# Splitting the mixer's per-head matrix work into pieces placed between the tiles of the next head's projection blocks

## What is computed

```
q, v, zf, zb, g = split(h @ w_in, 5)           # q = silu(q); k = (1-lb) * sigmoid(-z); f = lb + (1-lb) * sigmoid(z)
cum    = cumsum(log f) inside chunks of 64     # 12 chunks
scores = tri * ((q * exp(cum - ref)) @ (k * exp(ref - cum)).T)        # inside a chunk
kv[n]  = (k * exp(last - cum)).T @ v           # one 128 x 128 product per chunk
s[n+1] = decay[n] * s[n] + kv[n]               # chain over the chunks, both directions
o      = scores @ v + (q * exp(cum)) @ s[n]
y      = o * rsqrt(mean(o*o) + eps) * gnorm * silu(g)
out    = y @ w_out
```

## Time and profile before

| | |
|---|---|
| time, median of 3 runs | 3496.42 us |
| the profiled execution | 3493.21 us, span 3491.5 us |
| TensorE busy | 3158.1 us (90%) |
| TensorE weight load busy | 2570.7 us (74%) |
| VectorE busy | 1861.7 us (53%) |
| ScalarE busy | 1387.5 us (40%) |
| mean granted TensorE clock | 0.947 |
| HBM traffic | 102 GB/s over the span |

### The profile page before, as it was taken

The page is one execution under the profiler, slowest core; times in us unless marked ns, Lnnn a source line. Parts: engine busy times, 40 slices in busy tenths (PEclk is TensorE's granted clock), DMA queues, the critical chain, the costliest instruction groups (busy, mean ns, idle before and its releaser), DMA issues.

```text
span 3491.5 us, 44906 instructions
## 1 busy us (share of the span) xinstructions
PE 3158.1 (90%) x16582; PEld 2570.7 (74%) x16582; DVE 1861.7 (53%) x2627; ACT 1387.5 (40%) x1905; POOL 116.1 (3%) x121
## 2 busy tenths in 40 slices
PE   5988888578996999899888999999998999889997
PEld 4777777467875888766776888878887778678886
DVE  6554555367985443678536534563446333454435
ACT  4445544446874222456314322342224332342222
POOL 0000000000000000043100000000000000000000
PEclk8999989698998999999998999999999999999998
DMA  4311211138992222221001222222222222123322
GB/s 170 127 55 57 70 54 54 37 120 337 390 359 83 96 96 96 85 71 61 23 2 61 96 96 96 102 88 97 93 95 97 73 73 90 50 71 103 101 97 73
DMA packets 98049, 357.66 MB, mean 102 GB/s; under 512 B 11008, under 2 KB 11392, under 8 KB 97536
## 3 DMA queue, kind: packets, MB, share of 16 engines
q1 hardware_dynamic: 92448, 334.54, 27.5%
q0 software_dynamic: 4176, 15.24, 1.2%
q10 hardware_dynamic: 1296, 6.11, 0.5%
HBM read 344.29 MB, written 11.56 MB: 102 GB/s over the span
## 4 chain that ended last, share of the span: by engine, by line
PE 78%; DVE 9%; ACT 7%; issue 4%; DMA 1%; POOL 0%; ACTq 0%; DVEq 0%; POOLq 0%
PE bank L281 20%; PE bank L282 19%; PE bank L283 19%; PE bank L1622 1%; PE bank L1624 1%; PE bank L1623 1%; PE gbank L920 1%; ACT whi L259 1%; PE bank L2603 1%; ACT L352 1%; DVE cum L1066 1%; PE gbank L902 1%; PE gbank L937 1%; PE bank L1651 1%; PE bank L1650 1%
## 5 line engine op out<-in xcount | busy, mean ns | idle before, releaser
L281 PE MATMUL bank<-h_hi_buf,whi 128*128 128x512 f32 x2320 | 929.5, 401 | 53.7 <-DVE h_lo_buf L450 33.9
L282 PE MATMUL bank<-h_lo_buf,whi 128*128 128x512 f32 x2320 | 912.6, 393 | 0.0
L283 PE MATMUL bank<-h_hi_buf,wlo 128*128 128x512 f32 x2320 | 911.0, 393 | 0.0
L259 ACT ACTIVATE whi<-raw 128x1024 fp32r<-128x1024 f32 x466 | 477.3, 1049 | 456.5 <-PE bank L283 402.3
L272 DVE TENSOR_TENSOR wlo<-raw,whi 128x1024 fp32r<-128x1024 f32 x444 | 533.4, 1221 | 138.6 <-ACT whi L259 71.8
L281 PEld LDWEIGHTS bank<-h_hi_buf,whi 128*128 128x128 f32 x2320 | 442.4, 191 | 167.5 <-DVE h_lo_buf L450 42.7
L282 PEld LDWEIGHTS bank<-h_lo_buf,whi 128*128 128x128 f32 x2320 | 442.2, 191 | 95.2 <-issue 5.3
L283 PEld LDWEIGHTS bank<-h_hi_buf,wlo 128*128 128x128 f32 x2320 | 441.4, 190 | 93.9
L281 PE MATMUL bank<-a_hi_buf,whi 128*128 128x512 f32 x960 | 377.1, 393 | 25.0 <-DVE a_lo_buf L3184 9.6
L282 PE MATMUL bank<-a_lo_buf,whi 128*128 128x512 f32 x960 | 375.7, 391 | 0.0
L283 PE MATMUL bank<-a_hi_buf,wlo 128*128 128x512 f32 x960 | 375.6, 391 | 0.0
(11 more groups left out here) (512 smaller groups left out, 3803.3 us busy)
## 6 DMA issues: line engine op xcount, KB each, us to landing
raw<-in_w SPq DMA_DIRECT2D x634, 512.0 KB, 3.4
x<-in_x ACTq DMA_DIRECT2D x2, 2048.0 KB, 10.8
sorted_rows<-zrow POOLq DMA_DIRECT2D x7, 514.0 KB, 8.4
xrow<-sorted_rows POOLq DMA_DIRECT2D x7, 514.0 KB, 7.5
sorted_y<-ysb POOLq DMA_DIRECT2D x7, 512.0 KB, 7.4
out<-x SPq DMA_DIRECT2D x8, 256.0 KB, 2.0
xc<-in_xc ACTq DMA_DIRECT2D x1, 1024.0 KB, 8.7
waup<-in_waup ACTq DMA_DIRECT2D x1, 256.0 KB, 5.2
```

The costliest lines, as they stand in the source:

```text
L259: act.activation(k.whi[:, g.slot, :], k.raw[:, g.slot, :], ACT.Copy).then_inc(k.split_hi, 1)
L281: pe.matmul(out, w_hi, hi, start=(t == 0), stop=False)
L282: pe.matmul(out, w_hi, lo, start=False, stop=False)
L283: return pe.matmul(out, w_lo, hi, start=False, stop=(t == tiles - 1))
```

## The change

1. **Pieces.** `pe_tokens` and `pe_states` are cut up: V turn, K turn forward, K turn backward, scores, states in three lots. The V turn stands between block 0 and the modulation block; the others are called from inside `pe_block`, between two tiles of QB, VB and GB. The output stays at the end of the turn.
2. **Norm one turn later.** A turn has a third head `f` = h-2. Its norm product stands inside block 0, its ScalarE and VectorE steps between the steps of head e. The gate is now multiplied in before the norm factor (`y_gated`). One more turn is written out ahead of the loop, one more (none, none, 7) behind it.
3. **Half rows.** `v_half` and its two copies are gone. The chunk product reads 64 rows of `ktok` and of `vtok`; the chunk's parity chooses the bank, and a lot holds both directions and signals once (N_KV 3, not 6).
4. **Order on VectorE and ScalarE.** Gate products go ahead of split 2, both scans ahead of the modulation reduce and split 3, kk and qq ahead of the take of ZB; the chain's first lot ahead of the take of VB. ScalarE makes all six sigmoids ahead of split 2, copies V after the logarithms, and split 6 goes ahead of the copies of K.

Core of the diff:

```diff
+        def at_first(t):
+            if h.n.reg is None and h.n.base == 0:
+                pe.wait_ge(k.h_ready, q.h - DC + t + 1)
+            if f is not None and t == 4:
+                self.pe_norm(k, q, f)
+        def at_query(t):
+            if e is not None and t in (4, 7):
+                self.pe_keys(k, e, 0 if t == 4 else 1)
+        def at_value(t):
+            if e is not None and t == 2:
+                self.pe_scores(k, e)
+            if e is not None and t == 6:
+                self.pe_states(k, e, 0)
+        def at_gate(t):
+            if e is not None and t in (0, 4):
+                self.pe_states(k, e, 1 if t == 0 else 2)
+        pe_block(k, g, DC, lat, more=(con, h.count(3, 0)), ready=at_first)
         if e is not None:
-            self.pe_tokens(k, e)
+            self.pe_values(k, e)
...
+        pe_block(k, g + QB, DC, lat, ready=at_query)
+        pe_block(k, g + VB, DC, lat, more=(con, h.count(3, 2)), ready=at_value)
+        pe_block(k, g + GB, DC, lat, ready=at_gate)
         if e is not None:
-            self.pe_output(k, q, e)
+            self.pe_output(k, e)
...
+    def pe_turn(self, k, e, n, src):
         pe = k.nc.tensor
+        for i, tiles in enumerate((range(4), range(4, 6))):
+            if n == 0:
+                wait(pe, k.o_taken, e.n)
+            else:
+                wait(pe, k.tok_copied, e.count(N_TOK, n + i - 1))
+            for j in tiles:
+                last = pe.transpose(k.gbank[i][:, (j - tiles[0]) * P:(j - tiles[0] + 1) * P], src(j), k.ident[:, :])
+            last.then_inc(k.gla_full, 1)
...
+    def pe_states(self, k, e, lot):
         pe = k.nc.tensor
+        if lot == 0:
+            wait(pe, k.tok_copied, e.count(N_TOK, N_TOK))
+            wait(pe, k.pt_ready, e.count(N_SC, N_SC))
+        else:
+            wait(pe, k.chain_step, e.count(2 * STEPS, 8 * lot))
+        for i, j in enumerate(range(4 * lot, min(4 * lot + 4, STEPS))):
+            for d in range(2):
                 c = CHAIN[d][j]
+                half = slice(CH * (c % 2), CH * (c % 2) + CH)
+                last = pe.matmul(k.gbank[c % 2][:, i * P:(i + 1) * P], k.ktok[half, d, c // 2, :], k.vtok[half, c // 2, :],
+                                 start=True, stop=True)
+        last.then_inc(k.gla_full, 1)
...
     def run(self, eng, k, q, iteration):
+        iteration(k, q, Head(0), None, None)
+        iteration(k, q, Head(1), Head(0), None)
+        iteration(k, q, Head(2), Head(1), Head(0))
+        with eng.Fori(0, HEADS - 3) as it:
+            iteration(k, q, Head(At(3, 1, it)), Head(At(2, 1, it)), Head(At(1, 1, it)))
+        iteration(k, q, None, Head(HEADS - 1), Head(HEADS - 2))
+        iteration(k, q, None, None, Head(HEADS - 1))
...
@@ act_iteration
+        if f is not None:
+            wait(act, k.o_taken, f.count(1, 1))
+            act.activation(k.osq[:, :], k.o32[:, :], ACT.Square).then_inc(k.osq_ready, 1)
...
+        if f is not None:
+            wait(act, k.norm_sum, f.n + (q.norm + 1))
+            act.activation(k.lnv[:, :], k.nbank[:, :], ACT.Ln, bias=k.eps_col[:, :], scale=1.0 / P).then_inc(k.ln_ready, 1)
+        if e is not None:
+            turned(0, k.vtok)
         split(3)
+        if f is not None:
+            wait(act, k.ln_ready, f.n + (q.norm + 1))
+            wait(act, k.y_ready, f.n)
+            act.activation(k.rstd[:, :], k.lnv[:, :], ACT.Exp, scale=-0.5).then_inc(k.rstd_ready, 1)
...
@@ dve_iteration
         split(2)
         if e is not None:
+            for d in range(2):
+                self.dve_scan(k, e, d)
         if h is not None:
             wait(dve, k.block_done, g + MOD_BLOCKS + 1)
             dve_mod(k, k.bank[1][:, 0:MOD_BLOCKS * P], MOD_BLOCKS, h.n.times(MOD_BLOCKS) + 2 * DC, 0,
...
         split(3)
...
+        take(ZB, k.z_st[:, 1, :], context=True)
+        split(4)
+        if f is not None:
+            wait(dve, k.rstd_ready, f.n + (q.norm + 1))
+            wait(dve, k.y_gated, f.count(1, 1))
+            dve.scalar_tensor_tensor(k.o32[:, :], k.o32[:, :], k.vec("gnorm")[:, 0:1], k.rstd[:, :], ALU.mult, ALU.mult
+                                     ).then_inc(k.y_ready, 1)
+        split(5)
...
+            self.dve_chain(k, e, 0)
         take(VB, k.v_st[:, :], context=True)
         if e is not None:
+            self.dve_chain(k, e, 1)
+            self.dve_chain(k, e, 2)
```

More of the change, by code:

```diff
@@ L861, in pe_iteration @@
         con = lambda t: k.hc[:, t, :]
[L862 to L870, removed]
@@ L871, in pe_iteration @@
-        if e is not None:
-            self.pe_tokens(k, e)
-        if h is not None:
-            pe_block(k, g + VB, DC, lat, more=(con, h.count(3, 2)))
-        if e is not None:
[L876 to L879, removed]
-            self.pe_output(k, q, e)
-    def pe_tokens(self, k, e):
-        pe = k.nc.tensor
[L885 to L897, removed]
+        if h is None:
+            if f is not None:
[3 more added lines that the diff above has]
+                for d in range(2):
+                    self.pe_keys(k, e, d)
+                self.pe_scores(k, e)
+                for lot in range(N_KV):
+                    self.pe_states(k, e, lot)
+                self.pe_output(k, e)
+            return
@@ L991, in act_iteration @@
         split(5)
+        split(6)
         if e is not None:
-            n = 0
             wait(act, k.exp_done, e.count(4, 4))
[L995 to L1008, removed]
+            turned(2, k.ktok[:, 0])
+        if f is not None:
+            wait(act, k.y_ready, f.count(1, 1))
+            act.activation(head_view(k.a_hi_buf, f.n), k.o32[:, :], ACT.Copy).then_inc(k.y_hi, 1)
+        if e is not None:
+            turned(4, k.ktok[:, 1])
+        split(7)
         if e is not None:
@@ new lines, in dve_chain @@
+    def dve_chain(self, k, e, lot):
+        dve = k.nc.vector
+        wait(dve, k.gla_full, e.count(G_HEAD, N_TOK + N_SC + lot + 1))
+        for j in range(4 * lot, min(4 * lot + 4, STEPS)):
+            for d in range(2):
+                if j > 0:
+                    wait(dve, k.chain_step, e.count(2 * STEPS, 2 * j + d - 1))
+                if j >= 5:
+                    wait(dve, k.state_copied, e.count(STATE_COPIES, 2 * (j - 5) + d + 1))
+                kv = k.gbank[CHAIN[d][j] % 2][:, (j % 4) * P:(j % 4 + 1) * P]
+                before = CHAIN[d][j - 1]
+                if j == 0:
+                    wait(dve, k.rho_done, e.count(2, 2))
+                    ins = dve.tensor_copy(k.xs[:, d, 0, :], kv)
+                else:
+                    ins = dve.scalar_tensor_tensor(k.xs[:, d, j % 2, :], k.xs[:, d, (j - 1) % 2, :],
+                                                   k.rho[:, d, before:before + 1], kv, ALU.mult, ALU.add)
+                ins.then_inc(k.chain_step, 1)
```

205 lines of the change are left out of this document (92 added, 113 removed).

## The result

The changed kernel takes 3371.5 us, median of four runs (3371.0 to 3376.4), against 3493.8 for the kernel before (four runs, 3488.2 to 3500.3): a ratio of 0.965 [0.963, 0.967]. The forecast was 3397 with a range of 3378 to 3420: the direction was right, the gain of 122 us was a quarter larger than the 99 I gave, and the time lies under the range.

What follows compares the result with a forecast made beforehand. TensorE and waits in its in-order work were taken to set the turn. Seven turns falling to 394.5 us (-93.4) and the tail (-6) took 3493.2 to 3393.8, or 3397 as median; range 3378 to 3420.

Steps and rivals of the forecast that it cites:

- part 2: States in half rows: 44 instructions at 0.107 us plus 0.2 for each of three pieces, 5.3 us a turn.
- the term for the half rows: States of a turn: 44 half-row instructions at 0.107 us each, without overlap, within 5.3 us.
- The second rival: States: half rows overlap, 2.35 us less a turn, 3381 us; chance 0.10 together with a better clock.
- The stall of 0.5: Waits of TensorE in a turn where margins are small: 0.5 us added, between 0 and 2.5.
- Three places with margins of 0.1 to 0.2: QB's weights, states lot 1 to 2, and lot 2 to output: not all hold, so 0.5 us a turn.
- Transposes and change-overs: In a turn, 18 transposes at 0.12, 2.2 us; changes from full-row f32 pieces back to blocks, 0.4 us.
- The margin at QB: Low part of QB's weights ready on VectorE at 22.3 us of the turn, wanted by TensorE at 22.5: 0.2.
- the 4.9 us set aside: Remainder of the old third turn of 69.68 us, put to half clock and restarts behind gaps.
- the end of -11: Tail, where only the last head's mixing is left: best case -11 us if its output gets full clock; -6 expected.
- VectorE's queue as the pace: Both scans ahead of QB's split make QB late every turn: 3411 us, 3425 with a clock dip; chance 0.22.
- The clock held down by f32 pieces: f32 pieces keep QB, VB, GB and output at 1.2 GHz: turn of 89 us, kernel about 3610; chance 0.03.
- Uncovered pieces: Waits inside the blocks as long as before, only moved: same turn, less the tail, 3490 us; chance 0.01.

Runs made afterwards that it cites:

- the first run above: Changed kernel with each lot of states issuing all products of the lower half of the rows, then all of the upper: 3388.8 us, 0.971 of the kernel before.
- the two copies: Changed kernel with two useless 512-column VectorE copies in every turn ahead of the low part of QB's weights: 3380.8 us, 0.967 of the kernel before.

## Why the forecast was right in its direction and too high

**The step that failed** is in part 2: "eight f32 instructions of 64 rows ... 0.86 us, 0.107 each" and the sentence built on it, "By the second the 44 would need 2.35; the 0.107 disagrees". The row has eight instructions and one shape, and I took it for eight of that shape. The line of the same instructions, asked by itself in the kernel before, shows two (min/median/max in ns, start, shapes):

```profile
L2121 PE MATMUL bank<-kv_a,q_a x8: 272/374/378, 1514.7 to 1515.3; 64*128 64x128 f32 x4, 64*128 64x256 f32 x4
```

Four of 128 columns and four of 256. As an estimate from the lots above, with overlap these are 4 x 0.056 + 4 x 0.11 + 0.2 for the first and last (1.09 - 16 x 0.056) = 0.86, which is what passed; without, 1.5. The row that disagreed with the Trainium skill (TensorEngine Tiling (Array Packing), Key Properties: tiles run matmuls in parallel) in truth agreed with it, and the first run above shows it with nothing but an order changed: pairs every 0.112 us against single instructions every 0.112 us. Another row of the kernel before had the number in the plain, in a layer that I didn't look at (TensorE in time order):

```profile
1699.66 1.16 PE L2597 MATMUL bank<-ar,bt_y 64*128 64x128 f32 x16
```

Sixteen in 1.16, as in the states after. So the step that failed is the term for the half rows, 44 x 0.107 = 4.7 of the 5.3: its instructions do overlap, and measured 0.059. The second rival was thus what happened, and it stood in the text with its price, 2.35 a turn, and a chance that was too small. Undone by the sorted order, it is 1.55, since some overlap is left there: 44 x (0.096 - 0.059) = 1.6. Without this one error the time would have lain inside the range, with all the others made: the sorted order takes 3388.8 us. Against full rows it is 44 x (0.112 - 0.059) = 2.3, of which the changes at the three lots take back a part, and 1.4 are left. That a change of the mode drains the engine is what the same section of the Trainium skill has. The 0.09 and 0.12 agree with it, though a full-row f32 piece, which changes no mode, is left at 0.08 too, so most of the 0.12 may not be the drain.

**The rest of the sum**, a turn of 53.7 against 56.5:
- *States* 5.3, measured 3.06 for the lots and 0.6 for the changes into and behind them: -1.6.
- *The stall of 0.5* "between 0 and 2.5": 0. "Three places with margins of 0.1 to 0.2 will not all hold" was a guess about small errors of one sign. QB held with 0.1. The chain's two places had more room than I counted: the four tiles between two lots take 2.93 (227.65 to 230.58), not 2.72, because the first product behind a piece is longer; the piece's own cost is the chain's cover.
- *Transposes and change-overs* 2.2 + 0.4: a V or K turn stands in 0.57 from its first transpose to the next product, where I had 6 x 0.12 = 0.73; the product behind is 0.08 longer, which for the V turn stands in the modulation's 4.24; -0.5 in all.
- *Scores* 1.9 and their change-over 0.1: measured 1.70 and a longer product behind; -0.2. *Norm* 1.0: 0.46 and 0.40 on the product behind it, -0.1. *Output* 5.3: 5.27. *The blocks* 39.9: right; modulation 4.24, context 2.80, block 5.46.

**What was right.** The waits are gone, and by the reason given: in the same kernel with the steps whole those for the chain and for ScalarE's copies return (+7.7 us a turn), with the norm in its turn that for osq (+4.7), with VectorE's old order that for kk (+1.3). Full rows cost +1.4 without a wait. These add up to 15.1, beside 16.0 us between 69.7 and 53.7 (17.0 from the mean of 70.7); parts undone one at a time need not add up, and the place of the V turn was not undone by itself. The margin at QB is what the walk gave. The clock was 1.00 in the turns. With 5.7 us of waits it was 0.94 and the turn 7.7 longer, so I read the 4.9 us set aside "to the stretch at half clock and to restarts" as going with the waits; with the norm in its own turn, 4.0 us of waits cost 4.7 at a clock of 1.00. The tail came to 58.1 for "near 59", with its output at 0.50: the end of -11, at the full clock, asks for products that fill the waits.

**The rivals.** VectorE's queue as the pace (0.22) is refuted for this kernel and is 0.1 us away from being true, as the two copies show; with the norm in its own turn it happens. The clock held down by f32 pieces (0.03) is refuted at 1.00. Uncovered pieces (0.01) are refuted. **The range** failed for a reason of its own: its low end of 3378 took change-overs at nothing or overlapping rows, not both. 3381 for the rows less 7 x 1.2 for the small terms gives 3372.6; the 3371.5 measured is 1.1 below even that, which is less than the 5 us between the slowest and the fastest of the four runs. Independent errors of one sign add; a bound has to hold them together.

## What to carry to other kernels

Cut a chained step into pieces of 1 to 2 us and put them between the tiles of work that needs nothing from it: here this brought 7.7 us a turn, and 1 us of wait was worth 1.35 where the clock fell with it, 1.2 where it didn't. Where the contraction is over 64 rows, order the products so that neighbours stand in different halves (and here also in different banks), and expect the gain only where what feeds them is not the pace: alone on the old order it brought 0.4% of the time. Before a duration of a merged row goes into a sum, split it by shape, and look for a second place in the trace that has the same shape alone.

## What the runs showed of the hardware that I had not expected

- f32 instructions of 128 columns start 0.112 us apart with 128 rows, and 0.112 apart with 64 rows as long as they stay in one half. With both halves in turn, two start together every 0.112. The averages over a lot, 0.059 and 0.096, hold the first step and the passage between the halves.
- A piece with 64 rows costs 0.09 to enter and 0.12 to leave beyond the block's own pace of 0.23; a full-row f32 piece leaves at 0.08 and enters at nothing.
- The 10 us output of the last head, f32 of 64 and 128 columns without a gap, ran at a granted clock of 0.50, which is the 1.2 GHz level; ahead of it TensorE had waited for 2.4 us. With 7 products of 512 columns ahead of it and a wait of 0.6, it ran at 1.00 to its end and took 5.35 us.
- A VectorE copy of 128 x 512 f32 within the state buffer takes 0.42 us and the next operation starts 0.33 behind it; from the accumulators the same copy takes 0.69.
